# Two attention stages of a transformer pair: scores issued for both heads of a pair, score blocks in joint groups, last heads spread over a longer stretch of the output projection

## The reference

```python
# first block, heads of 64; c is the running sum of the log forget gates
logits = q @ k.T * scale + c[query] - c[key]          # causal
p = softmax(logits);  out = p @ v
# second block, per head two score maps m of depth 64 and values of width 128
scores = einsum('bqhmd,bkhmd->bhmqk', qb, kb) + alibi_bias
probs = softmax(scores);  weights = probs[:, :, 0] - lam * probs[:, :, 1]
o = rms_norm(weights @ v, head_norm_g) * (1 - lam_0) * silu(z)
return x + o @ w_out                                   # w_out: 2048 x 1024
```

## Time and profile before

| what | value |
|---|---|
| time, 3 runs | median 1353.13 us (1349.94 to 1353.45) |
| the profiled execution | 1352.76 us, of which the span from first to last instruction is 1351.0 us |
| PE busy | 1330.9 us (99%) |
| DVE, ACT, POOL busy | 774.8 us (57%), 617.9 us (46%), 355.0 us (26%) |
| mean granted clock of TensorE | 0.993 |

### The profile page before, as it was taken

One profiled execution on the slowest core, in us unless ns is written; L12 is line 12 of the kernel. 1 busy time (PEld: TensorE's weight loads), 2 busy tenths in 40 slices (PEclk: granted clock), 3 DMA queues, 4 the chain that ended last, 5 costly groups with the idle time before them and its releaser, 6 DMA issues.

```text
span 1351.0 us, 18430 instructions
## 1 busy us (share of the span) xinstructions
PE 1330.9 (99%) x7206; PEld 1097.0 (81%) x7206; DVE 774.8 (57%) x1536; ACT 617.9 (46%) x1315; POOL 355.0 (26%) x245
## 2 busy tenths in 40 slices
PE   7999999999999999999999999999999999999999
PEld 6777777888879999999888787877777777777787
DVE  4415556433559888887424646466666656567632
ACT  4325555322435444445324446455556555556620
POOL 3012220000026565560001413141323324143300
PEclk8999999999999999999999999999999999998999
DMA  6302122222261432333235321322222222321331
GB/s 239 102 23 79 48 84 72 94 94 94 94 233 48 156 94 94 125 109 111 63 125 202 108 65 63 102 71 71 80 93 71 70 71 70 102 78 63 126 125 63
DMA packets 110103, 130.87 MB, mean 97 GB/s; under 512 B 7488, under 2 KB 87360, under 8 KB 110016
## 3 DMA queue, kind: packets, MB, share of 16 engines
q1 hardware_dynamic: 104400, 112.39, 25.7%
q10 hardware_dynamic: 5616, 17.30, 3.3%
HBM read 120.24 MB, written 9.44 MB: 96 GB/s over the span
## 4 chain that ended last, share of the span: by engine, by line
PE 89%; DVE 5%; ACT 3%; issue 1%; POOL 1%; DMA 0%; ACTq 0%; POOLq 0%; DVEq 0%
PE ps L797 15%; PE ps L799 14%; PE ps L798 14%; PE ps L802 7%; PE ps L804 6%; PE ps L803 6%; PE ps L997 5%; PE ps L1000 5%; PE ps L999 5%; PE ps L1052 3%; DVE wlo L1410 2%; PE ps L1062 1%; PE ps L1037 1%; ACT px L1361 1%; PE ps L1086 1%
## 5 line engine op out<-in xcount | busy, mean ns | idle before, releaser
L1410 DVE TENSOR_TENSOR wlo<-raw,whi 128x512 fp32r<-128x512 f32 (+1 forms) x262 | 224.1, 880 | 207.9 <-ACT whi L1115 207.3
L1115 ACT ACTIVATE whi<-raw 128x512 fp32r<-128x512 f32 (+2 forms) x338 | 210.0, 649 | 149.4 <-PE ps L799 96.0
L797 PE MATMUL ps<-whi,hth 128*128 128x512 f32 x592 | 249.3, 421 | 2.7 <-DVE wlo L1410 2.7
L799 PE MATMUL ps<-wlo,hth 128*128 128x512 f32 x592 | 232.9, 393 | 0.0
L798 PE MATMUL ps<-whi,htl 128*128 128x512 f32 x592 | 232.0, 392 | 0.0
L1800 POOL TENSOR_TENSOR wlo<-raw,whi 128x512 fp32r<-128x512 f32 (+1 forms) x76 | 90.4, 1204 | 444.7 <-ACT whi L1115 444.7
L797 PEld LDWEIGHTS ps<-whi,hth 128*128 128x128 f32 x592 | 111.8, 189 | 35.0 <-issue 9.5
L799 PEld LDWEIGHTS ps<-wlo,hth 128*128 128x128 f32 x592 | 111.5, 188 | 25.7
L798 PEld LDWEIGHTS ps<-whi,htl 128*128 128x128 f32 x592 | 112.1, 189 | 17.7
L1361 ACT ACTIVATE px<-px,nm 128x128 f32<-128x128 f32 (+3 forms) x128 | 71.0, 556 | 106.0 <-DVE nm L1719 106.0
L802 PE MATMUL ps<-hth,whi 128*128 128x512 f32 (+1 forms) x288 | 114.8, 399 | 0.0
(11 more groups left out here) (338 smaller groups left out, 2962.7 us busy)
## 6 DMA issues: line engine op xcount, KB each, us to landing
raw<-in_l_w_in SPq DMA_DIRECT2D x64, 512.0 KB, 4.7
raw<-in_w_gate_up SPq DMA_DIRECT2D x44, 512.0 KB, 4.7
raw<-in_w_in SPq DMA_DIRECT2D x14, 1024.0 KB, 5.2
raw<-in_w_down SPq DMA_DIRECT2D x10, 1024.0 KB, 5.0
raw<-in_l_w_out SPq DMA_DIRECT2D x8, 1024.0 KB, 5.0
raw<-in_w_in SPq DMA_DIRECT2D x24, 256.0 KB, 3.6
raw<-in_w_branch SPq DMA_DIRECT2D x8, 512.0 KB, 3.9
raw<-in_w_out SPq DMA_DIRECT2D x4, 1024.0 KB, 5.0
```

Of the source, the lines that this page charges most:

```text
L797: e.matmul(o, ah, wh[:, cs], start=a, stop=False)
L799: m = e.matmul(o, ah, wl[:, cs], start=False, stop=z)
L1115: return e.activation(out, in_, ACT.Copy, **how)
L1410: return e.tensor_tensor(out, src, hi_part.bitcast(F32), ALU.subtract)
```

## The change

- **First attention.** `attn1` works on pairs of heads (2j, 2j+1). `sc` has three events per pair, query blocks (0, 1), (2) and (3); each issues the three passes alternately for the two heads, rows 0 to 63 and 64 to 127, into two banks. The two `rb` of the next pair follow, then four empty yields, then the transposes two by two and `pv`. The generator has 62 yields instead of 91 over the same 60 sub-units. `rb` uses 128 rows instead of 8: `id8` and `ctb` are widened, with zeros below row 8 (a new memset on POOL ahead of the first step).
- **Second attention.** `s2` has three events per head instead of four: blocks 0 and 1 share one event and one pair of banks. A slot has nine yields instead of ten. `ga` writes into the first bank of the `s2` of the same slot, once its scores are consumed, instead of a bank of its own.
- **Last heads.** Slots 14 to 16 are spread (36 yields) over the 48 sub-units of both column halves, k = 0 to 2. Both halves accumulate in `PJ`; after k = 2 `yo` adds the bank to `xo`, which frees it, and k = 3 of both halves is a fresh accumulation with a second `yo`. `xb` moves to between slots 14 and 15; the fourth residual buffer is one of its own.

```diff
-        merge(self.conv_and_gates(), 60, self.attn1(), 8 * 10 + 11)
+        merge(self.conv_and_gates(), 60, self.attn1(), 2 + 4 * 15)
...
-            merge(self.proj2(g + 1), 32, self.slots(2 * g, 2 * g + 2), 20)
-        gen = self.slots(14, 17)
-        advance(gen, 2)
-        merge(self.w2_first(), 24, gen, 24)
-        put("xb")
-        self.spare = [TBK[1]]
-        finish(self.w2_units(1, 0, [0]))
-        self.gate2()
-        finish(self.w2_units(1, 0, [1]))
-        put("to", 15, self.bank())
-        finish(self.w2_units(1, 0, [2, 3]))
-        for c, k in ((1, 1), (1, 2), (0, 3), (1, 3)):
-            finish(self.w2_units(c, k))
+            merge(self.proj2(g + 1), 32, self.slots(2 * g, 2 * g + 2), 18)
+        merge(self.w2_first(), 48, self.last_heads(), 36)
+        for c in range(2):
+            finish(self.w2_units(c, 3))
...
     def attn1(self):
+        put = self.put
+        put("rb", 0, self.bank())
+        yield
+        put("rb", 1, self.bank())
+        yield
+        for j in range(H1 // 2):
+            for ev in range(3):
+                put("sc", j, ev, self.bank(), self.bank())
+                if ev:
+                    put("dv", j, ev - 1)
+                yield
+            for h in (2 * j + 2, 2 * j + 3):
+                if h < H1:
+                    put("rb", h, self.bank())
+                if h % 2 == 0:
+                    put("dv", j, 2)
+                yield
+            for _ in range(4):
+                yield
+            for h in (2 * j, 2 * j + 1):
+                for kb in range(TB):
+                    put("tu", h, kb, self.bank())
+                    if kb % 2:
+                        yield
+                yield
+                put("pv", h, self.bank())
...
     def slot(self, h):
...
         if now:
-            put("s2", h, 0, self.bank(), self.bank())
+            b = self.bank()
+            put("s2", h, 0, b, self.bank())
             yield
-        self.gate2()
+        self.gate2(b)
...
+    def last_heads(self):
+        yield from self.slot(14)
+        self.put("xb")
+        yield from self.slot(15)
+        yield from self.slot(16)
+        yield
+        yield
+        self.gate2()
+        for _ in range(3):
+            yield
+        self.put("to", 15, self.bank())
+        yield
...
-            if k == 3:
-                self.put("yo", c, tb)
+            if k >= 2:
+                self.put("yo", c, k, tb)
...
     def w2_first(self):
-        for k in range(3):
-            yield from self.w2_units(0, k)
+        for c in range(2):
+            for k in range(3):
+                yield from self.w2_units(c, k)
...
-                    l8 = id8[:, h:h + 1].to_broadcast([H1, P])
-                    e.matmul(ps[b][:, :], l8, cth, start=True, stop=False)
-                    e.matmul(ps[b][:, :], l8, ctl, start=False, stop=True).then_inc(rb_pe, 1)
+                    l8 = id8[:, h:h + 1].to_broadcast([P, P])
+                    e.matmul(ps[b][:, :], l8, ctb[:, 0:S], start=True, stop=False)
+                    e.matmul(ps[b][:, :], l8, ctb[:, S:2 * S], start=False, stop=True).then_inc(rb_pe, 1)
...
-                    e.matmul(o, qh[r, j, qs], kh[r, j, 0:n], start=True, stop=False)
-                    e.matmul(o, qh[r, j, qs], kl[r, j, 0:n], start=False, stop=False)
-                    e.matmul(o, ql[r, j, qs], kh[r, j, 0:n], start=False, stop=True).then_inc(sc_pe, 1)
+                    for qb in QBS1[ev]:
+                        n = P * (qb + 1)
+                        c, qs = P if qb == 1 else 0, slice(P * qb, n)
+                        for i in range(3):
+                            for m in range(2):
+                                r, o = slice(64 * m, 64 * m + 64), ps[(b0, b1)[m]][:, c:c + n]
+                                mark = e.matmul(o, (ql if i == 2 else qh)[r, j, qs], (kl if i == 1 else kh)[r, j, 0:n],
+                                                start=i == 0, stop=i == 2)
...
+            e.memset(ctb[:].bitcast(F32), 0.0).then_inc(ctb_made, 1)
```

More of the change, by code:

```diff
@@ L360, in attn1 @@
     def attn1(self):
[L361 to L375, removed]
+        put = self.put
[21 more added lines that the diff above has]
+                    if kb % 2:
                         yield
-            if h + 1 < H1:
-                self.put("rb", h + 1, self.bank())
                 yield
[L380 to L384, removed]
+                put("pv", h, self.bank())
     def block_end(self, blk, nA, after, ahead):
@@ L466, in proj2, with gate2 @@
                 yield
-    def gate2(self):
+    def gate2(self, b=None):
         if self.og_wait:
-            self.put("ga", self.og_wait.pop(), self.bank())
+            self.put("ga", self.og_wait.pop(), self.bank() if b is None else b, 0)
     def slot(self, h):
@@ L490, in slot @@
             yield
+        if now:
+            put("s2", h, 1, self.bank(), self.bank())
+            put("cb", h, 1)
+            yield
         if out:
             put("to", h - 2, self.bank())
[L493 to L496, removed]
             yield
@@ L503, in slot @@
         if now:
-            put("s2", h, 3, self.bank(), self.bank())
+            put("s2", h, 2, self.bank(), self.bank())
             put("cb", h, 2)
@@ L617, in build @@
         sq2 = [both(att, f"sq2{i}", [P, S]) for i in range(3)]
-        qn = [both(att, f"qn{i}", [P, S]) for i in range(3)]
+        qn = [both(att, "qn0", [P, S])]
+        with ExitStack() as c:
+            xo3 = sbuf(c, "xo3", [P, D])
+        qn += [both(att, f"qn{i}", [P, S]) for i in (1, 2)]
         pth2 = sbuf(att, "pth2", [P, CAUSAL], F32R)
@@ L1046, in _ @@
                     claim(b1)
[L1047 to L1054, removed]
+                    for qb in QBS[ev]:
+                        n = P * (qb + 1)
+                        c, qs = P if qb == 1 else 0, slice(P * qb, n)
+                        for i in range(3):
+                            for m in range(2):
+                                r, o = slice(64 * m, 64 * m + 64), ps[(b0, b1)[m]][:, c:c + n]
+                                left = (qkl if i == 2 else qkh)[i2][r, hh, qs]
+                                right = (qkl if i == 1 else qkh)[i2][r, 2 + hh, 0:n]
+                                mark = e.matmul(o, left, right, start=i == 0, stop=i == 2)
+                                if i == 2 and qb == QBS[ev][-1]:
+                                    mark.then_inc(s2_pe, 1)
                     for m in range(2):
-                        free[(b0, b1)[m]] = [(max2_d, 8 * h + 2 * qb + m + 1)]
+                        free[(b0, b1)[m]] = [(max2_d, 8 * h + 2 * QBS[ev][-1] + m + 1)]
                 elif kind == "t2":
@@ L1085, in _ @@
                     for qb in range(TB):
-                        m = e.matmul(ps[b][:, qb:qb + 1], osq[:, P * qb:P * qb + P], ones[:, 0:1], start=True, stop=True)
+                        m = e.matmul(ps[b][:, c + qb:c + qb + 1], osq[:, P * qb:P * qb + P], ones[:, 0:1], start=True, stop=True)
                     m.then_inc(ss_pe, 1)
@@ L1355, in _ @@
                 elif kind == "s2":
-                    h, qb, b0, b1 = a
-                    for m in range(2):
-                        sl = px[2 * (h % 2) + m][:, QSEG[qb]:QSEG[qb] + P * (qb + 1)]
-                        c = 8 * (h % 2) + 2 * qb + m
-                        act.wait_ge(max2_d, 8 * h + 2 * qb + m + 1)
-                        e.activation(sl, sl, ACT.Exp, bias=nm2[:, c:c + 1], scale=-1.0,
-                                     accum_out=ls2[:, c:c + 1]).then_inc(exp2_a, 1)
+                    h, ev, b0, b1 = a
+                    for qb in QBS[ev]:
+                        for m in range(2):
+                            sl = px[2 * (h % 2) + m][:, QSEG[qb]:QSEG[qb] + P * (qb + 1)]
+                            c = 8 * (h % 2) + 2 * qb + m
+                            act.wait_ge(max2_d, 8 * h + 2 * qb + m + 1)
+                            e.activation(sl, sl, ACT.Exp, bias=nm2[:, c:c + 1], scale=-1.0,
+                                         accum_out=ls2[:, c:c + 1]).then_inc(exp2_a, 1)
                 elif kind == "cb":
```

172 lines of the change are left out of this document (97 added, 75 removed).

## The result

The changed kernel takes **1336.01 us** (median of 4 runs, 1335.83 to 1338.37) against 1353.24 us for the kernel before in runs beside it: a ratio of 0.9886, 95% interval 0.9874 to 0.9898, or 17 us less. The forecast was 1325 (1317 to 1338). The time lies inside the range, but in the stretch that belonged to the first rival: the range held because it had been drawn wide enough to take in most of that rival. Some 10 us of the gain are missing.

A forecast was written before the change was run, and what follows sets the result against it. The prediction took PE, busy 1330.9 of 1351.0 us, as the bound. Its terms, -7.6 - 9.2 - 6.4 + 0.5 + 1.5 - 6.3 = -27.5 us, took 1352.8 to 1325.3, stated as 1325, range 1317 to 1338.

The forecast's parts named there:

- the first rival: Waits at `ga`, at `xb` or in too dense last heads replace the gain: 1331.6 to 1339 us; chance 0.13.
- Scores in pairs: First attention: two heads' score matmuls run at once, halving 15.3 us of PE; 7.6 us gained, bounds 0 and 7.6.
- Borders of the first attention: First attention: 46 fewer changes of row count on PE at 0.20 us each; 9.2 us gained, lower bound 0.
- End of the first attention: Late transposes of the last heads hold up ACT and `pv`: two stalls of 0.75 us, 1.5 us lost, bounds 0 and 5.
- The slower rival: First attention: PE reaches a pair's transposes before both heads are scaled; at 9 us late, 1361 us; chance 0.03.
- Borders of the second attention: Second attention: joint score groups cut 128 borders to 96, 0.20 us each; 6.4 us gained, lower bound 0.
- `ga` in the score bank: Second attention: `ga` newly waits for DVE's maxima, 0.7 us of cover left; 0.5 us lost in all.
- in the other slots of that parity it is the same: Second attention: the 0.7 us of cover for `ga`, worked out in slot 7, also holds in slots of that parity.
- `xb`, nothing: Last heads: ACT stops at `xb` for POOL's `og`, some 6 us, but readers come later; costs nothing, uncovered 6 us.
- The last heads: Last heads: spreading over 48 sub-units puts `ga` further behind its `p2`; 6.3 us gained, bounds 0 and 7.3.
- 7.3 us of waits and slow clock should fall to about 1: Last heads: PE's three longest waits, 4.2 us, plus 3.1 us lost at half clock shrink to about 1 us.
- The signs and the range: Trace signs of being right, such as a slot pair shorter by 0.8 us, and the range 1317 to 1338 us.

The follow-up runs named there:

- e9: Kernel before plus only the first attention's edits, with both heads of a pair computed from the first head's rows: 1343.40 us, ratio 0.9939.
- e10: Kernel before plus only the first attention's edits, with `rb` taken back to 8 rows: 1338.47 us, ratio 0.9898.
- e3: Changed kernel with `to` back before the second score group, at sub-unit 8 instead of 9: 1335.34 us, ratio 0.9881.
- e6: Changed kernel with the second score group two sub-units later, at 11, behind `to` and the first single transposes: 1334.70 us, ratio 0.9869.
- e2: Changed kernel with a bank of its own for `ga`, one more claim per slot: 1333.70 us, ratio 0.9864.
- e4: Changed kernel with the edits of e2 and e3 together: 1333.07 us, ratio 0.9861.
- e5: Changed kernel with `xb` two yields later, behind the third step of slot 15: 1330.76 us, ratio 0.9836.
- e11: Changed kernel with the order of e6 in slots 0 to 13, the bank of e2 from slot 14 on, and `xb` as in e5: 1331.03 us, ratio 0.9843.
- e8: Kernel before plus only the first attention's edits, with one head's three passes written before the other's: 1336.71 us, ratio 0.9887.

## Why the prediction was right in one half and wrong in the other

- **Scores in pairs, -7.6.** Right. e9 takes the neighbour away and loses 7.5 us in the stage (7.7 between the medians).
- **Borders of the first attention, -9.2.** Right. The stage gained 15.5 us against -7.6 - 9.2 + 1.5 = -15.3, and e10 gives back 16 borders for 3.0 us in the stage where 3.2 was due. The trace has 70 and 24 borders, as counted; that the other 30 cost the same follows from the sum alone. The rule of the Trainium skill ("TensorE: Matmul & The Clock Gate", Part 3) that the prediction weighed against the `rb` edit did not show: with weight loads of their own its matmuls start 0.23 us apart, and the 2.9 us did not come.
- **End of the first attention, +1.5.** Of the right kind: `pv` waits for `ptl`, 0.6 us in the list of waits. Each of the two late starts is some 0.45 us where I had put 0.75.
- **The slower rival** did not happen: no wait on the pair's chain, and a clock of 1.00 in the stage.
- **Borders of the second attention, -6.4.** Mis-sized: about 0.9 us came between `qt` 0 and `qt` 7, where 5.1 were due (12.75 heads at 0.4 us). The borders went, but the step counted matmuls only and left out what moves with them: 18 yields over 32 sub-units in another order. `to` stands one sub-unit later, ACT stands at the DMA behind it until DVE has written `ots`, and the exponentials of block 2 now stand ahead of the square that leads to `qn_f`; so `qt` starts 0.30 us late in each group. `p2` claims a bank that `qt` had and starts 0.4 us late. e3 and e6 cut the first wait to 0.09 and 0.05 us by the order alone and give back 0.9 and 1.1 us over four groups, 0.2 to 0.3 each, as its size says. That the second wait holds the other 1.6 us is read from the timeline; no run took it away.
- **`ga` in the score bank, +0.5.** The step "in the other slots of that parity it is the same" failed. It held in slots 0 to 13, where no wait of `ga` shows. In slots 14 and 15 DVE has weight splits ahead of the maxima, and `ga` waits 2.7 and 0.9 us, the first with 3.4 us at 1.2 GHz behind it. Taking the shared bank away (e2) gives 2.8 us in the stretch, though more by the clock than by the waits.
- **`xb`, nothing.** Failed, and it was named with its price: uncovered 6 us. I looked for splits and distant readers behind it; what mattered was ACT's copy of transposes, which empties a bank: in e4 its late end holds the next scores for 2.5 us. ACT stood for 7.60 us, and moving it gave 2.4 us in the stretch (e5).
- **The last heads, -6.3.** The step "7.3 us of waits and slow clock should fall to about 1" failed. The waits for squares and `og` did go, but the two items above took their place, and the slow clock came back behind them: waits and slow clock are 8.1 us of the stretch before and 8.8 after. Forecast was a last stretch of 156.1 - 7.6 = 148.5 us with about 1 us of that left; the best of the runs (e11) has 152.6 with no slow clock and 4.2 us of waits, so 3.2 of the 4.1 us between them are waits.
- **The signs and the range.** The 24 borders, three `s2` groups per head and `rb` at 0.23 us were there. The shorter pair of slots, the clock without 0.50 in the last heads and `ga` without a wait on DVE were not. The lower end of the range is also added wrongly: 1325.3 less 0.5 + 1.5 of waits, 1.0 of the 7.3 us and 3.5 of spread is 1318.8, not 1317.

So the first rival, that waits take the place of the gain, is what happened beside a right main term, in the last heads by both of the ways named there, and in the slots by others than `ga`. I gave it 0.13 because I had checked the cover in one slot in the middle. The median of e5 is 5 us lower where the stretch is only 2.4 shorter. The clock accounts for most of the rest: a mean granted clock lower by 0.001 stands for some 1.3 us lost over a run of this length; the changed kernel's four executions had 0.992 to 0.993, and those of e5 took 1334.29, 1332.35, 1329.09 and 1329.17 us at 0.994, 0.995, 0.997 and 0.997. What stays open is why a wait is followed by the slow clock in one execution and not in another, and so how much of these 5 us e5's edit earned.

## What to carry to other kernels

On an engine that is always busy, count the distance between starts: here a change of row count cost 0.19 to 0.20 us where it was measured, and two matmuls on different row groups cost one. When several edits share four rotating banks, a gain in matmuls is only as good as the order of the claims: list who had the bank before and what empties it, in each kind of slot. Check cover at the ends of a loop, where other work shares the engine, and look twice before you put DMA issues that wait for a far result into the queue of an engine that empties banks. When kernels differ by a few us, read the granted clock of each stretch before you credit an edit.

## What the runs showed of the hardware that was not expected

Order does not make the pair. Three accumulating matmuls on rows 0 to 63 followed by three on rows 64 to 127 ran side by side from the start, 0.01 us apart (e8, 106.190 and 106.200 us), and eight heads took the same 309.6 us as with the passes interleaved. A short wait of PE can be dearer than its length, and not each time: 2.3 us behind a wait of 2.66 us the granted clock fell to 0.50 for 3.4 us, 1.7 us more; one wait of 2.1 to 2.2 us in the gate's part, in code that some of these kernels share, was followed by 3.4 us at 0.50 in seven of thirteen profiled executions and by none in the other six.
